# One trunk step on one core: gate half pieces a unit ahead, query and key transposes in the idle gate bank, output projection by halves

## What is computed

```python
def trunk_layer(x, cond, lp, lambda_init, rope, ctx_kv):
    m = jax.nn.silu(cond) @ lp['w_ada'] + lp['b_ada']
    shift1, scale1, gate1, shift2, scale2, gate2 = jnp.split(m[:, None, :], 6, axis=-1)
    h = rms_norm(x, lp['norm1_g']) * (1.0 + scale1) + shift1
    mix, k, v = token_mixer(h, lp, lambda_init, rope, ctx_kv)
    x = x + gate1 * mix
    h2 = rms_norm(x, lp['norm2_g']) * (1.0 + scale2) + shift2
    x = x + gate2 * expert_choice_moe(h2, ...)

def token_mixer(h, ...):
    q, k, v, zu, zv, g_a, g_b = split(h @ w_in)
    o_a = diff_attention(q, k_all, v_all, lam)
    o_a = rms_norm(o_a, subln_g) * (1.0 - lambda_init)
    o_b = spatial_gating(zu, zv, ...)
    merged = jax.nn.sigmoid(g_a) * o_a + jax.nn.sigmoid(g_b) * o_b
    return merged @ w_out, k, v
```

## Time and profile before

| | |
|---|---|
| runs (3), median, lowest, highest | 1911.86, 1911.29, 1915.69 us |
| the profiled execution, its own time | 1914.82 us |
| its span, first to last instruction | 1913.0 us |
| mean granted clock of TensorE, share of full | 0.967 |
| busy: PE, DVE, ACT, POOL | 1780.6, 1438.0, 1110.3, 383.3 us |
| chain that ended last | PE 88%, DVE 4%, ACT 3%, DMA 2% |
| HBM read, written | 485.90, 19.42 MB |

### The profile page before, as it was taken

The page is one execution under the profiler, slowest core; times in us unless marked ns, Lnnn a source line. Parts: engine busy times, 40 slices in busy tenths (PEclk is TensorE's granted clock), DMA queues, the critical chain, the costliest instruction groups (busy, mean ns, idle before and its releaser), DMA issues.

```text
span 1913.0 us, 23998 instructions
## 1 busy us (share of the span) xinstructions
PE 1780.6 (93%) x8609; PEld 1253.5 (66%) x8609; DVE 1438.0 (75%) x1404; ACT 1110.3 (58%) x1159; POOL 383.3 (20%) x202
## 2 busy tenths in 40 slices
PE   5899999988888969499999999999999999999996
PEld 2677787766776757366666666666666666666664
DVE  1588636355555566789999998998899889899895
ACT  2443322255555631277777777777777777777773
POOL 1264403000000000103303312321330331132021
PEclk9899999999989979599999999999999999999998
DMA  9245633312122042499999999999999999999993
GB/s 321 98 146 199 233 126 131 106 65 80 44 71 71 11 176 100 162 345 372 383 384 379 378 387 381 378 383 382 376 381 382 377 377 384 379 378 384 382 375 118
DMA packets 264866, 506.13 MB, mean 265 GB/s; under 512 B 10284, under 2 KB 29956, under 8 KB 264808
## 3 DMA queue, kind: packets, MB, share of 16 engines
q1 hardware_dynamic: 256248, 483.38, 69.7%
q0 software_dynamic: 8560, 21.98, 4.4%
HBM read 485.90 MB, written 19.42 MB: 264 GB/s over the span
## 4 chain that ended last, share of the span: by engine, by line
PE 88%; DVE 4%; ACT 3%; DMA 2%; issue 1%; SPq 1%; POOL 0%; DVEq 0%; ACTq 0%; POOLq 0%
PE banks L1491 26%; PE banks L1492 26%; PE banks L1493 26%; PE banks L1670 2%; PE banks L1582 2%; DMA raw<-in_w_ada 1%; PE banks L1510 1%; PE banks L1771 1%; PE banks L1657 1%; ACT w_hi L663 1%; DVE w_lo L922 1%; PE banks L1738 1%; PE banks L1758 1%; PE banks L1621 0%; PE banks L1524 0%
## 5 line engine op out<-in xcount | busy, mean ns | idle before, releaser
L1349 DVE TENSOR_TENSOR w_lo<-raw_x,w_hi 128x2048 fp32r<-128x2048 f32 x192 | 437.5, 2286 | 65.5 <-ACT w_hi L900 63.7
L1349 DVE TENSOR_TENSOR w_lo<-raw,w_hi 128x2048 fp32r<-128x2048 f32 x189 | 431.0, 2287 | 35.2 <-ACT w_hi L900 31.5
L900 ACT ACTIVATE w_hi<-raw 128x2048 fp32r<-128x2048 f32 x189 | 362.9, 1920 | 110.6 <-PE banks L1493 109.2
L900 ACT ACTIVATE w_hi<-raw_x 128x2048 fp32r<-128x2048 f32 x192 | 368.1, 1917 | 85.5 <-PE banks L1493 84.1
L1491 PE MATMUL banks<-w_hi,xe_hi 128*80 128x512 f32 x1024 | 406.0, 397 | 2.2 <-issue 2.2
L1492 PE MATMUL banks<-w_hi,xe_lo 128*80 128x512 f32 x1024 | 403.9, 394 | 0.0
L1493 PE MATMUL banks<-w_lo,xe_hi 128*80 128x512 f32 x1024 | 400.1, 391 | 0.0
L1467 POOL DMA_INDIRECT out<-yeg,idx_l x32 | 146.4, 4576 | 831.9 <-DVE yeg L1311 831.9
L1491 PE MATMUL banks<-w_hi,h_hi 128*128 128x512 f32 x560 | 230.4, 411 | 22.4 <-DVE w_lo L922 20.0
L1493 PE MATMUL banks<-w_lo,h_hi 128*128 128x512 f32 x560 | 223.8, 400 | 0.0
L1492 PE MATMUL banks<-w_hi,h_lo 128*128 128x512 f32 x560 | 223.4, 399 | 0.0
(11 more groups left out here) (207 smaller groups left out, 2064.2 us busy)
## 6 DMA issues: line engine op xcount, KB each, us to landing
raw<-in_w_gate_e SPq DMA_DIRECT2D x80, 1024.0 KB, 7.6
raw_x<-in_w_down_e SPq DMA_DIRECT2D x80, 1024.0 KB, 7.6
raw<-in_w_up_e SPq DMA_DIRECT2D x64, 1024.0 KB, 7.5
raw_x<-in_w_up_e SPq DMA_DIRECT2D x64, 1024.0 KB, 7.7
raw_x<-in_w_gate_e SPq DMA_DIRECT2D x48, 1024.0 KB, 6.1
raw<-in_w_down_e SPq DMA_DIRECT2D x48, 1024.0 KB, 8.0
raw<-in_w_in SPq DMA_DIRECT2D x28, 1024.0 KB, 5.1
raw<-in_w_ada SPq DMA_DIRECT2D x24, 1024.0 KB, 7.5
```

Of the source, the lines that this page charges most:

```text
L900: nc.scalar.activation(w_hi[:, j % NSPLIT], raw_slot(slot), ACT.Copy).then_inc(hi_done, 1)
L1349: nc.vector.tensor_tensor(w_lo[:, j % NSPLIT], raw_slot(EXPERT_SLOT[j % NRAWE]), w_hi[:, j % NSPLIT], ALU.subtract).then_inc(lo_done, 1)
```

## The change

- **Gate bank.** Query and key transposes inside the loop no longer go to bank 4 but to that one of banks 6 and 7 in which no gate is being filled (`head_bank`, `gates_of`). A transpose waits for the last group of its own kind only; a q/k group also waits until the gate in its bank has been read (`gate_out`); a half piece that opens a bank waits until all q/k groups have been taken.
- **Half pieces a unit ahead.** Unit u issues `half_piece(u + 1)`; unit 0 issues piece 1, unit 39 none. `gate` moves to even units, `gated` to odd ones.
- **Weights a unit sooner.** `hi` of the next block's chunks stands at the end of units 7 and 8 of each ten, `lo` at the end of 8 and 9; both chunks of the first `w_out` block so come inside the loop.
- **Root in two parts.** The head norms' root is taken for tiles 0 and 1 ahead of outputs 37 to 39, and for the others at a new step Q, with which ACT also splits the second `w_out` block; DVE's low parts of it are steps B 0 and B 1.
- **Projection by halves.** A W tile can be split: `BEFORE` names the step ahead of which PE issues its first 12 matmuls. `STEPS` has a new order. `xw`'s halves alternate. SP's two expert loads move behind the fourth x2 load.

```diff
 def head_bank(n):
-    return 6 if n < GROUPS_QK else 4
+    if n < GROUPS_QK:
+        return 6
+    return 4 if TRANSPOSED[n][0] == "a" else 6 + (gates_of(QK_UNIT[of_kind(n, "qk")]) + 1) % 2
...
+def gates_of(u):
+    return (u + 1) // 2
...
-STEPS = [("M", 0), ("T", 0), ("M", 1), ("T", 1), ("W", 0, 0), ("M", 2), ("W", 1, 0), ("M", 3), ("W", 0, 1), ("N", 0), ("R", 0), ("T", 2), ("M", 4),
-         ("W", 1, 1), ("N", 1), ("R", 1), ("T", 3), ("X", 0), ("W", 2, 0), ("W", 2, 1), ("N", 2), ("R", 2), ("L", 0), ("T", 4), ("X", 1),
-         ("W", 3, 0), ("W", 3, 1), ("N", 3), ("R", 3), ("L", 1), ("X", 2), ("W", 4, 0), ("L", 2), ("X", 3), ("L", 3), ("A", 0),
-         ("K", 0), ("K", 1), ("K", 2), ("W", 4, 1), ("K", 3), ("N", 4), ("K", 4), ("R", 4), ("K", 5),
-         ("X", 4), ("K", 6), ("L", 4), ("K", 7), ("A", 1), ("K", 8), ("K", 9)]
+STEPS = [("M", 0), ("T", 0), ("M", 1), ("T", 1), ("Q", 0), ("W", 0, 0), ("M", 2), ("T", 2), ("W", 1, 0), ("B", 0), ("M", 3), ("T", 3), ("W", 2, 0),
+         ("B", 1), ("M", 4), ("T", 4), ("W", 3, 0), ("W", 4, 0), ("W", 0, 1), ("W", 1, 1), ("N", 0), ("R", 0), ("X", 0), ("W", 2, 1), ("N", 1), ("R", 1),
+         ("L", 0), ("X", 1), ("W", 3, 1), ("N", 2), ("R", 2), ("L", 1), ("X", 2), ("N", 3), ("R", 3), ("X", 3), ("W", 4, 1), ("L", 2), ("L", 3), ("A", 0),
+         ("K", 0), ("N", 4), ("K", 1), ("K", 2), ("R", 4), ("K", 3),
+         ("X", 4), ("K", 4), ("K", 5), ("L", 4), ("K", 6), ("K", 7), ("A", 1), ("K", 8), ("K", 9)]
+BEFORE = {("T", 1): ("W", 0, 0), ("T", 2): ("W", 1, 0), ("T", 3): ("W", 2, 0), ("T", 4): ("W", 3, 0), ("X", 3): ("W", 4, 1)}
+EARLY_TILES = 2
...
-                if t == 2:
+                if t == NT - 1:
                     for i in (1, 2):
                         sp.wait_ge(lo_done, SPLIT_AT[PRE - 3 + i] + 1)
                         load_expert(i)
...
-                if u % 2 == 1:
+                if u % 2 == 0:
                     gate(u // 2)
...
-                if u % HALVES == HALVES - 1:
+                if u % HALVES == HALVES - 3:
                     hi(2 * (FIRST_B + u // HALVES + 1))
-                if u % HALVES == 0 and u >= HALVES:
-                    hi(2 * (FIRST_B + u // HALVES) + 1)
-            hi(PRE - 3)
-            for u in range(NU - 3, NU):
-                if u >= NU - 2:
-                    copy_out(transposed_upto("a", u))
+                if u % HALVES == HALVES - 2:
+                    hi(2 * (FIRST_B + u // HALVES + 1) + 1)
+            take_root(roots[0], H * EARLY_TILES)
+            roots[0] += 1
+            output(NU - 3)
+            for u in range(NU - 2, NU):
+                copy_out(transposed_upto("a", u))
                 output(u)
-            take_root(roots[0], H * NT)
-            roots[0] += 1
-            hi(PRE - 2)
-            hi(PRE - 1)
...
+                elif what == "Q":
+                    take_root(roots[0], H * (NT - EARLY_TILES), H * EARLY_TILES)
+                    roots[0] += 1
+                    hi(PRE - 2)
+                    hi(PRE - 1)
...
-                if u >= 2 and u % 2 == 0 and u // 2 - 1 < 3 * NT:
-                    gated(u // 2 - 1)
+                if u % 2 == 1 and u // 2 < 3 * NT:
+                    gated(u // 2)
                 for g in qk:
                     qk_low(GROUP_AT[g[:3]])
+                if u % HALVES == HALVES - 2:
+                    lo(2 * (FIRST_B + u // HALVES + 1))
                 if u % HALVES == HALVES - 1:
-                    lo(2 * (FIRST_B + u // HALVES + 1))
-                if u % HALVES == 0 and u >= HALVES:
-                    lo(2 * (FIRST_B + u // HALVES) + 1)
+                    lo(2 * (FIRST_B + u // HALVES + 1) + 1)
             combine(NU - 1)
-            lo(PRE - 3)
...
+            def heads_root(first, last):
+                c = slice(first * H, last * H)
+                dve.wait_ge(osq_ready, NU - NT + last)
...
+            heads_root(0, EARLY_TILES)
...
+                    dve.wait_ge(og_ready, NU - NT + t + 1)
...
-                    if t == 1:
-                        lo(PRE - 2)
-                        lo(PRE - 1)
+                elif what == "Q":
+                    heads_root(EARLY_TILES, NT)
+                elif what == "B":
+                    lo(PRE - 2 + t)
...
-                    if n >= 1:
-                        before = TRANSPOSED[n - 1][0]
-                        pe.wait_ge(tr_emptied[before], of_kind(n, before))
+                    if of_kind(n, what):
+                        pe.wait_ge(tr_emptied[what], of_kind(n, what))
+                    if what == "qk" and n >= GROUPS_QK:
+                        pe.wait_ge(gate_out, gates_of(QK_UNIT[of_kind(n, "qk")]))
...
+                if half == 0 and m >= 1:
+                    pe.wait_ge(tr_emptied["qk"], of_kind(done[0], "qk"))
...
-                if u >= 1:
-                    half_piece(u)
+                if u + 1 < N_HALF:
+                    half_piece(u + 1)
...
+            def output_half(step, i):
+                _, t, j = step
+                b, place = FIRST_WO + j, P2.index((*step,))
+                ps = bank(place % RING)
+                n = 2 * b + i
+                if i == 0:
+                    if place >= RING:
+                        pe.wait_ge(p2_emptied, place - RING + 1)
+                    pe.wait_ge(p2_emptied, P2.index(("T", t, 1)) + 1)
...
             for what, t, *half in STEPS:
+                if (what, t) in BEFORE:
+                    output_half(BEFORE[what, t], 0)
...
+                    step = (what, t, *half)
+                    if step not in BEFORE.values():
+                        output_half(step, 0)
+                    output_half(step, 1)
```

More of the change, by code:

```diff
@@ L202, in of_kind @@
     return sum(1 for p in TRANSPOSED[:n] if p[0] == what)
+QK_UNIT = [None] * GROUPS_QK + [_u for _u in range(NU) for _ in unit_groups(_u)[1]]
+def gates_of(u):
+    return (u + 1) // 2
 def head_bank(n):
-    return 6 if n < GROUPS_QK else 4
+    if n < GROUPS_QK:
+        return 6
+    return 4 if TRANSPOSED[n][0] == "a" else 6 + (gates_of(QK_UNIT[of_kind(n, "qk")]) + 1) % 2
 SG_STEP = {4 * fb + 2: fb for fb in range(4)}
@@ L1158, in _ @@
                     combine(u - 1)
[L1159 to L1160 removed]
+                if u % 2 == 1 and u // 2 < 3 * NT:
+                    gated(u // 2)
                 for g in qk:
                     qk_low(GROUP_AT[g[:3]])
+                if u % HALVES == HALVES - 2:
+                    lo(2 * (FIRST_B + u // HALVES + 1))
                 if u % HALVES == HALVES - 1:
[L1164 to L1166 removed]
+                    lo(2 * (FIRST_B + u // HALVES + 1) + 1)
             combine(NU - 1)
[L1168 to L1175 removed]
+            def heads_root(first, last):
+                c = slice(first * H, last * H)
+                dve.wait_ge(osq_ready, NU - NT + last)
+                nc.vector.tensor_scalar(var[:, c], var[:, c], 1.0 / VD, EPS, ALU.mult, ALU.add).then_inc(var_ready, 1)
+                dve.wait_ge(var_ready, rooted[0] + 1)
+                finish_root((last - first) * H, c=first * H)
+            heads_root(0, EARLY_TILES)
             n2 = [0]
@@ L1210, in _ @@
                     c = slice(half * CW, (half + 1) * CW)
-                    nc.vector.tensor_tensor(xw[:, c], ps, gate1[:, int(t == NL), c], ALU.mult).then_inc(p2_emptied, 1)
+                    s = (t + half) % 2
+                    own = xw[:, s * CW:s * CW + CW]
+                    nc.vector.tensor_tensor(own, ps, gate1[:, int(t == NL), c], ALU.mult).then_inc(p2_emptied, 1)
                     dve.wait_ge(p2_emptied, n2[0])
-                    last = nc.vector.tensor_tensor(x2[:, t, c], x2[:, t, c], xw[:, c], ALU.add)
+                    last = nc.vector.tensor_tensor(x2[:, t, c], x2[:, t, c], own, ALU.add)
                     if half == 1:
@@ L1703, in piece2 @@
                 return bank(n % RING)
+            def output_half(step, i):
[7 more added lines that the diff above has]
+                    pe.wait_ge(p2_emptied, P2.index(("T", t, 1)) + 1)
+                if t == 0:
+                    pe.wait_ge(lo_done, SPLIT_AT[n] + 1)
+                for k in range(CK):
+                    kk = i * CK + k
+                    last = split3(ps, m_hi[:, t, kk, :], m_lo[:, t, kk, :], w_hi[:, split_slot(n), k, :],
+                                  w_lo[:, split_slot(n), k, :], kk == 0, kk == KT - 1)
+                if i == 1:
+                    n2[0] += 1
+                    last.then_inc(p2_done, 1)
             for what, t, *half in STEPS:
+                if (what, t) in BEFORE:
+                    output_half(BEFORE[what, t], 0)
                 if what == "T":
@@ L1714, in _ @@
                 elif what == "W":
-                    pe.wait_ge(p2_emptied, P2.index(("T", t, 1)) + 1)
-                    b = FIRST_WO + half[0]
-                    if t == 0:
-                        pe.wait_ge(lo_done, SPLIT_AT[2 * b + 1] + 1)
-                    ps = piece2()
-                    for n in (2 * b, 2 * b + 1):
```

(9 more changed lines are left out.)

5 lines of the change are left out of this document (removed).

## The result

The changed kernel takes **1891.89 us** (median of 4 runs, 1888.88 to 1893.44), the kernel before, run beside it, 1911.57 (4 runs, 1910.66 to 1915.69): a ratio of 0.9891, 95% interval [0.9871, 0.9911]. The forecast was 1892.3, a gain of 19.5 us; the gain was 19.7. The profiled execution took 1890.38 us, its span is 1888.5, against 1914.82 and 1913.0 before.

A forecast was written before the change was run, and what follows sets the result against it. TensorE, busy 93% of the span, bounds the kernel, so only its idle time and low-clock losses can be had. Terms: -1.8 - 14.7 - 16.4 - 9.1 + 25.5 - 3.0 = -19.5 us, from 1911.86 to 1892.3; range 1878 less 1, up to 1907.

The forecast's parts named there:

- 1, start: Start of attention: half piece 1 fills the first wait, PE idles 1.9 us not 4.7, low clock behind goes: -1.8 us.
- 2, queries and keys: Attention: with queries and keys in the gate bank, probabilities' transposes no longer wait for them: -14.7 us.
- 3, weights a unit sooner: Attention: six waits for new weights become three of 3.0 us, with fewer falls of the clock: -16.4 us.
- 4, tail: Attention's tail: first w_out splits and half piece 39 leave it, root taken earlier; +14.5 instead of +23.6 us: -9.1 us.
- 5, projection: Output projection with router: VectorE's order makes PE wait 21 us, three clock falls add 8.4: +25.5 us in all.
- 6, choice of tokens: Choice of tokens: DVE no longer closes or awaits W4,1 there, and the last router step comes sooner: -3.0 us.
- 7, nothing: Expert loads moved behind four x2 loads, and alternating xw halves: no effect on the time.
- A: Rival, attention and projection: no clock fall after waits of 3.0 us and none after the 3.8: 1878 us, 20%.
- B: Rival, attention: exponentials hold it, so the queries and keys part gives a third only: 1902 us, 16%.
- C: Rival, projection: PE stays at the low clock through most of it: 1957 us if all, 1920 if half, 7%.
- D: Rival, projection: DVE's order costs another 14 us over the forecast's 17, cancelling the gains: 1907 to 1914 us, 7%.

The follow-up runs named there:

- the old order: Changed kernel with the step list of the kernel before, steps Q and B set in behind T 1, and whole W tiles: 1868.37 us.
- whole-tile kernel: Changed kernel with its new step order but whole W tiles, no half issued ahead of T1 to T4 and X3: 1909.81 us.
- one swap of two operations: Changed kernel with the first w_lo of a new gate block ahead of the low keys on VectorE in units 8, 18, 28: 1882.52 us.
- the first execution without the half: Changed kernel with old step order and new weights ahead of low keys, no half of W 0,0 ahead of T 1: first measured at 1857.34 us.

## Why the prediction was right, and where its steps were off

The time, 1892.3 against 1891.9, is right by its own mechanisms: the lengths of attention, tail, projection and choice were each within 1.4 us of the forecast. That it is right to half a microsecond is luck. The lengths all erred to the same side: between the two profiled executions the gain is 24.5 us and not 19.5. The medians, which the forecast was for, have 19.7; the profiled execution of before lay 3.2 us above its median and that of after 1.5 below. For the profiled execution the forecast was 1895.3, and it took 1890.38.

- *1, start* (-1.8). PE's wait for the first exponentials fell from 4.7 to 1.7 us (forecast 1.9), and unit 1 took 4.7 us (387.73 to 392.42) where it had taken 6.5 (388.77 to 395.28): 1.8 us. With the gate bank alone unit 1 took 6.4, with bank 4 and the half piece ahead 4.7, so it is the half piece.
- *2, queries and keys* (-14.7). Measured by taking it back: 9.7 us of attention, some 11 with as many falls of the clock. The step that failed was "units of 128 queries and keys 0 to 767 ... nothing": units 13, 23 and 33 wait 0.49 us each, 1.5 in all. The rest of the gap was not an error of the sum, since part 3 charged the longer wait for weights in full: 3.5 us of what this part frees is taken up there (8.4 against 4.9).
- *3, weights a unit sooner* (-16.4). Three waits of 2.8 us at units 9, 19, 29 (forecast 3.0) and none in 10 and 11. The clock term was right by errors that cancel: after the change three falls and not two, of 1.6 us and not 2.8, 4.8 for 5.6; before it four falls, as the prediction has it, but the one of unit 21 cost 1.5 and not 2.8 (the unit took 11.3 us, units 11 and 31 12.6 and 12.5), 9.9 for 11.2. So the term saved 5.1 us where 5.6 were forecast. How much hangs on the sooner renewal was not priced: it is worth 32 us once the half pieces are ahead, and without it the change would have been a loss.
- Attention by the three parts: forecast 246.8 from first scores to scores 39, measured 245.5.
- *4, tail* (-9.1). 13.9 us where 14.5 was forecast, in this execution. The 2 us "for the low level" are no constant: see the last section. No run takes the tail's parts back one by one, so its causes are read from the waits: the 2.58 us between the last outputs are gone.
- *5, projection* (+25.5). 104.1 us against 105.0. Waits: T 2 2.06 (forecast 2.4), T 3 and T 4 3.88 and 3.87 (3.8), X 0 3.70 (3.8), X 1 and X 2 2.01 (1.9), X 3 1.73 (1.7), the first half 1.81 (1.7): 21.1 for 21. The cause, VectorE's order, is shown by the old order (78.8 us), and for X 0 by moving norm 0. The clock was put at 8.4 for three falls, one behind each wait of 3.8. Taking waits (21.1), work (72.7) and the end (2.9) from 104.1 leaves 7.4: the size is about right, and the step behind it is wrong. Only two of the three waits of 3.8 were followed by the low level, the 3.70 at X 0 was not, and the waits of 1.81 and 2.06 were. That the term came out is luck.
- *6, choice of tokens* (-3.0): -3.6.
- *7, nothing*: not tried alone; what follows the choice differs by 0.7 us.

The rivals: A (the clock kinder) fails, with 0.98 in attention and 0.89 in the projection. It was right in part: the wait of 3.70 us at X 0 cost no clock, nor did the 2.81 of unit 19 in the old-order kernel; and with no wait of over 0.6 us but the first (1.7) attention runs at 1.00. B (held by exponentials): no wait for them but the first. Its mark, units over 6.7 us outside the three, did show in four (6.9 us in unit 3, 7.3 in 13, 23, 33), but with 0.49 us of waits for keys at most and the rest PE's own work, so the mark was set too low. C (low level through the projection) fails at 0.89. It leaned on the Trainium skill ("TensorE: Matmul & The Clock Gate", section "A second HAM failure mode: psum-queue depth-cycling"), which has the clock swing where PE idles briefly and often between groups that cycle through the PSUM banks. This trace agrees for the first 44 us after the first product (0.81) and not for the next 50, which have four such waits in the same ring of six banks and stand at 1.00. Nor does the sum of waits set the level alone: the ring was at 0.91 in the old order with 9.5 us of waits and at 0.80 in the whole-tile kernel with 36.6, but at 0.87, 0.89, 0.89 and 0.92 in four kernels with the changed projection and 22.5 to 23.6 us of waits, and at 0.85 with norm 0 moved and 5.5 us less. D (another 14 us of VectorE's queue) fails: the waits came to 21.1. The kernel without halves shows such a case: 13 us more of waits, 1909.8.

## What to carry to other kernels

A list of steps that all engines walk in order is priced on the engine that is *not* the bound: add up what VectorE must do between two steps of TensorE, and the waits come out to within 0.4 us (eight of them here). A change of several parts can hide a loss in one of them as large as half its gain, so time its stages apart and try the old form of each; here two small edits, the old order and one swap of two operations, gave some 34 us on top of 20. And work moved ahead needs its inputs moved as far ahead: half pieces put one unit sooner with their weights left a unit later cost 32 us.

## What the runs showed that had not been expected

- The same instructions with nearly the same waits take different times by the clock alone. The tail (unit 39's scores to the first transpose of o_t) has the waits of 2.03 and 0.90 us and three short ones, equal to 0.2 us, in every version with the changed tail, and took 12.53 us at a granted clock of 1.00, 13.9 at 0.88, 15.1 at 0.77 and, in the first execution without the half, 15.98 at 0.68; the same program gave 15.98 in one execution and 15.06 in another. The projection of the changed kernel did the same, 101.1 us at 0.92 (in the kernel with bank 4) to 105.0 at 0.87. So a step worth less than some 3 us is not settled by medians of four runs, nor by its stage in one execution: the waits show it.
- A fall of the clock behind a wait for weights cost 2.8 us three times and 1.5 once before the change, and 1.6 three times after it. Where it cost 2.8, all twelve matmuls of the half piece were at the low level; where it cost 1.5 or 1.6, the first few still went at the high one and seven or eight at the low. So the price depends on how much work meets the low level, and "one fall, one price" is good to a factor of two.
- The length of a wait did not decide whether the clock falls. In the changed kernel all three waits of 2.81 us in attention were followed by the low level, in the old-order kernel two of the same three, and before the change one of three of 3.2 us. In the projection a wait of 1.81 us was, and one of 3.70 was not. What does decide it stays open.
